# A hybrid decoder layer on one core: the first transfers of the kernel in another order

## The chip, the cores and the metric

The kernel runs on one core of a Trainium2 chip. The metric is the device time of one execution in microseconds (us); the median over several runs is compared. A profile of one execution is read beside it. Its span runs from the first to the last instruction.

## What is computed

The reference is one decoder layer on x of 512 rows and 1024 features: a norm, a mixer with two branches (block-sparse attention and a gated delta rule), a residual, a second norm and a squared-ReLU MLP. What matters here is its beginning only:

```
def rms_norm(x, w):
    y = x * rsqrt(mean(x * x, axis=-1) + 1e-6)
    return y * w

h = rms_norm(x, pre_norm_mix)          # x: 512 x 1024
proj = h @ w_in                        # w_in: 1024 x (3600 + 2 * 1024) columns
...                                    # attention, delta rule, merge, w_out
x = x + rms_norm(y, post_norm_mix)
y = square(relu(rms_norm(x, pre_norm_mlp) @ w_mlp_in)) @ w_mlp_out
return x + rms_norm(y, post_norm_mlp)
```

## The kernel before

Every float32 product is made from three: each operand is split into a high part (rounded to the matmul's own format) and a low part (what is left), and TensorE adds high by high, high by low and low by high. ScalarE makes the high part of each weight tile (`w_hi`), VectorE or GpSimd the low part (`w_lo`). The weights of the projection come in 88 "units" of 256 KB; a unit covers 256 columns for two chunks of 128 features. They go through four buffers `raw[0]` to `raw[3]`.

x comes transposed, in eight chunks of 128 features by 512 rows (`x_t[:, k, :]`, 256 KB each, 2048 bytes for a partition). The norm's weight `wpre` (one column for each chunk, 4 KB in all) is multiplied in before the projection, the row scale after it. So for each chunk k, ScalarE makes `h_hi(k) = x_t * wpre` rounded (`h_part`, L1113 through `copy`), and VectorE makes `h_lo(k) = x_t * wpre - h_hi(k)` (L1492).

The beginning is ordered by hand:

- SP's queue (L555 to L563): chunk 0 of x, the first half of unit 0 (semaphore `w0_in`), the second half of unit 0, and then, for u from 1 to 3, unit u and chunks 2u and 2u + 1. After these come unit 4 and those behind it, with x in its own order (`x_sb`, four transfers) and the small vectors between them.
- ScalarE's queue (L1116, L1117): `wpre`, then chunk 1 of x. Behind these two, ScalarE loads its table and runs one activation on a flag. Then it waits for `wpre`, makes `h_hi(0)`, `h_hi(1)`, the second half of `w_hi` of unit 0, and for each u from 1 to 3 `w_hi` of unit u, `h_hi(2u)`, `h_hi(2u + 1)`.
- VectorE casts the first half of unit 0 itself (L1508), makes its low part, and goes on with `h_lo(0)`, the low part of the second half, `h_lo(1)`, and so on.
- TensorE first runs eight matmuls on a tile of ones (`keep_warm`, L933; the profile counts 16 passes), and then `first_unit(u)`, which takes one chunk at a time: a pair of matmuls on `w_hi` and `h_hi` (L697), a pair on `w_lo` and `h_hi` (L703), a pair on `w_hi` and `h_lo` (L706). From unit 4 on, `unit(u)` waits for the whole unit's low part, which GpSimd makes for most units (L1961).

Of the kernel before, what the change touches and what calls it, by code (L numbers as in the profile page):

```python
# [16 lines left out]
F32 = mybir.dt.float32  # L17
F32R = mybir.dt.float32r
ALU = mybir.AluOpType
# [3 lines left out]
P = 128  # L23
D = 1024
S = 512
NT = S // P
KD = D // P
# [163 lines left out]
    return [(name, i) for u, name, i in STEPS if min(u, U_DN) == unit]  # L191


def program(nc, x, x_by_feature, small_vectors, pre_norm_mix, w_in, w_branch_att, w_branch_dn, w_out,
            post_norm_mix, w_mlp_in, w_mlp_out, post_norm_mlp, out):
    ctx = ExitStack()
    base = (nc.sbuf_base + 63) // 64 * 64
# [2 lines left out]
    def at(name, kb, shape, dt=F32):  # L200
        return nc.alloc_sbuf_tensor_at(name, shape, dt, offset=base + int(kb * KB))


    h_hi = at("h_hi", 0, [P, KD, S], F32R)
    h_lo = at("h_lo", 16, [P, KD, S], F32R)
    raw = at("raw", 32, [P, RAW, 512])
    w_hi = at("w_hi", 40, [P, SPL, 512], F32R)
    w_lo = at("w_lo", 48, [P, SPL, 512], F32R)

    x_t = at("x_t", 56, [P, KD, S])  # L210
    x_sb = at("x_sb", 112, [P, NT, D])
    gate_a = at("gate_a", 56, [P, KD, S])
    qk_dn = at("qk_dn", 72, [P, 8, S])
# [65 lines left out]
    def small(name, shape, dt=F32):  # L279
        n = 4  # L280
        for d in shape[1:]:
            n *= d
        t = nc.alloc_sbuf_tensor_at(name, shape, dt, offset=base + off[0])
        off[0] += (n + 31) // 32 * 32
        return t
# [5 lines left out]
    wpre = small("wpre", [P, KD])  # L291
# [45 lines left out]
    def sem(name):  # L337
        return ctx.enter_context(nc.semaphore(name))

    x_in = [sem(f"x_in{t}") for t in range(NT)]  # L340
    xt_in = [sem(f"xt_in{k}") for k in range(KD)]
# [11 lines left out]
    wpre_in = sem("wpre_in")  # L353
# [3 lines left out]
    w0_in = sem("w0_in")  # L357
# [7 lines left out]
    hhi_ready = sem("hhi_ready")  # L365
    hlo_ready = sem("hlo_ready")
# [108 lines left out]
    def unit_source(u):  # L475

        if u < U_IN:
            g = UNIT_GROUP[u]
            col, kind = GROUPS[g]
            j = u - TABLE[g][0]  # L480
            if kind == "f":
                return w1[j * 256:(j + 1) * 256, col:col + 256].rearrange("(k p) c -> p k c", p=P)
            return w1[j * P:(j + 1) * P, col:col + 512]
        if u < U_BR:
            j = u - U_IN
            w, g = (w_branch_att, w_branch_dn)[j // 8][0], j % 8 // 2
            return w[j % 2 * 256:j % 2 * 256 + 256, g * 256:g * 256 + 256].rearrange("(k p) c -> p k c", p=P)
        j = u - U_BR
        return w_out[0][j // 2 * P:j // 2 * P + P, j % 2 * 512:j % 2 * 512 + 512]
# [52 lines left out]
    def _(sp_):  # L542
# [8 lines left out]
        def load_xt(k):  # L551
            sp_.dma_start(x_t[:, k, :], x_by_feature[k * P:(k + 1) * P, :]).then_inc(xt_in[k], 16)

        load_xt(0)
        sp_.dma_start(raw[:, 0, 0:256], unit_source(0)[:, 0, :]).then_inc(w0_in, 16)  # L555
        sp_.dma_start(raw[:, 0, 256:512], unit_source(0)[:, 1, :]).then_inc(raw_in[0], 16)
        for u in range(1, 4):
            load(u, u, unit_source(u), None)
# [114 lines left out]
    def _(pe):  # L673
# [11 lines left out]
        def first_unit(u):  # L685

            first, banks, _, _ = TABLE[0]
            for kk in range(2):
                k = 2 * u + kk
                c = [slice(kk * 256 + m * P, kk * 256 + m * P + P) for m in range(2)]  # L690
                if k == 0:
                    pe.wait_ge(w0_hi, 1)
                else:
                    pe.wait_ge(hi_ready, u + 1)
                pe.wait_ge(hhi_ready, k + 1)
                for m in range(2):
                    pe.matmul(bank[banks[m]][:], w_hi[:, u, c[m]], h_hi[:, k, :], start=k == 0, stop=False, skip_group_check=True)  # L697
                if k == 0:
                    pe.wait_ge(w0_lo, 1)
                else:  # L700
                    pe.wait_ge(lo_ready, u + 1)
                for m in range(2):
                    pe.matmul(bank[banks[m]][:], w_lo[:, u, c[m]], h_hi[:, k, :], start=False, stop=False, skip_group_check=True)  # L703
                pe.wait_ge(hlo_ready, k + 1)
                for m in range(2):
                    i = pe.matmul(bank[banks[m]][:], w_hi[:, u, c[m]], h_lo[:, k, :], start=False, stop=k == KD - 1,  # L706
                                  skip_group_check=True)
            i.then_inc(unit_done, 1)

        def unit(u):  # L710
            s = u % SPL
            pe.wait_ge(lo_ready, u + 1)
            if u < U_IN:
                g = UNIT_GROUP[u]
                first, banks, _, need = TABLE[g]
                j = u - first
                if GROUPS[g][1] == "f":
# [377 lines left out]
    def _(a):  # L1095
        n = {}

        def mark(i, s):

            n[s.name] = n.get(s.name, 0) + 1  # L1100
            i.then_inc(s, 1)
            a.wait_ge(s, n[s.name])
# [9 lines left out]
        def copy(o, i_, scale=1.0):  # L1112
            return a.activation(o, i_, ACT.Copy, scale=scale)  # L1113


        a.dma_start(wpre[:], pre_norm_mix).then_inc(wpre_in, 16)  # L1116
        a.dma_start(x_t[:, 1, :], x_by_feature[P:2 * P, :]).then_inc(xt_in[1], 16)  # L1117
        a.wait_ge(flag_set, 1)
# [6 lines left out]
        def h_part(k):  # L1125

            a.wait_ge(xt_in[k], 16)
            mark(copy(h_hi[:, k, :], x_t[:, k, :], wpre[:, k:k + 1]), hhi_ready)

        def split(u, slot, loaded, used):  # L1130

# [10 lines left out]
            a.wait_ge(unit_done, U_DN)  # L1142
            copy(wx_hi[:, j, :], raw_x[:, j, :]).then_inc(hix_ready, 1)

        a.wait_ge(wpre_in, 16)
        h_part(0)
        h_part(1)
        a.wait_ge(raw_in[0], 16)
        copy(w_hi[:, 0, 256:512], raw[:, 0, 256:512]).then_inc(hi_ready, 1)
        for u in range(1, 4):  # L1150
            split_u(u)
            h_part(2 * u)
            h_part(2 * u + 1)
# [7 lines left out]
        def side_step(name, i):  # L1161
# [24 lines left out]
            elif name == "sg":  # L1186
                a.wait_ge(conv_done, i + 1)
                dst = qk_dn[:, i, :] if i < 8 else v_dn[:, i - 8, :]
                mark(a.activation(dst, dst, ACT.Silu), silu_done if i < 8 else silu_v_done)
            elif name == "ev" and i in (10, 11):  # L1190
                first, banks, _, _ = TABLE[i]
                for m, b in enumerate(banks):
                    if m < NT - 1:
# [281 lines left out]
    def _(v):  # L1475
        n = {}

        def mark(i, s):
            n[s.name] = n.get(s.name, 0) + 1
            i.then_inc(s, 1)  # L1480
            v.wait_ge(s, n[s.name])
# [9 lines left out]
        def stt(o, i0, s, i1, op0, op1):  # L1491
            return v.scalar_tensor_tensor(out=o, in0=i0, scalar=s, in1=i1, op0=op0, op1=op1)  # L1492
# [7 lines left out]
        def w_lo_part(u, c=slice(0, 512)):  # L1500
            return v.tensor_tensor(w_lo[:, u, c], raw[:, u, c], w_hi[:, u, c].bitcast(F32), ALU.subtract)

        def h_part(k):
            v.wait_ge(hhi_ready, k + 1)
            mark(stt(h_lo[:, k, :], x_t[:, k, :], wpre[:, k:k + 1], h_hi[:, k, :].bitcast(F32), ALU.mult, ALU.subtract), hlo_ready)

        v.wait_ge(w0_in, 16)
        mark(v.tensor_copy(w_hi[:, 0, 0:256], raw[:, 0, 0:256]), w0_hi)  # L1508
        mark(w_lo_part(0, slice(0, 256)), w0_lo)
        v.wait_ge(wpre_in, 16)  # L1510
        h_part(0)
        v.wait_ge(hi_ready, 1)
        w_lo_part(0, slice(256, 512)).then_inc(lo_ready, 1)
        h_part(1)
        for u in range(1, 4):
            v.wait_ge(hi_ready, u + 1)
            w_lo_part(u).then_inc(lo_ready, 1)
            h_part(2 * u)
            h_part(2 * u + 1)
# [13 lines left out]
        def side_step(name, i):  # L1533
# [28 lines left out]
            elif name == "b2":  # L1562
                s3 = [sp[:, q, :] for q in range(6)]
                for c in (9, 7, 5, 3):
# [6 lines left out]
                         alog.unsqueeze(1).to_broadcast([P, NT, H]), ALU.mult, ALU.mult), g_ready)  # L1571
            elif name == "ev" and i not in (10, 11):
                first, banks, _, _ = TABLE[i]
                v.wait_ge(unit_done, first + 4)
                if i == 14:
# [565 lines left out]
```

## Time and profile before

| | |
|---|---|
| time, median of 3 runs | 753.74 us (753.39 to 754.31) |
| the profiled execution | 753.69 us |
| its span | 751.9 us |
| TensorE busy | 744.5 us (99%) |
| VectorE, ScalarE, GpSimd busy | 418.1, 383.9, 322.6 us |
| mean granted TensorE clock | 0.998 |

An engine's busy time counts its own instructions; TensorE's weight loads are counted apart, since they run beside its matmuls. A timeline row gives the start, the length, the engine and line, what is written from what, the count of merged instructions and, in brackets, how long the engine had been idle and what ended that. SPq and ACTq are the queues on which SP and ScalarE issue transfers; the length of such a row is that of the issue alone.

### The profile page before, as it was taken

Reading aid. Unit: us, or ns where it says so; the run is one execution under the profiler, and the core shown is the slowest. Engines: PE = TensorE matmul, PEld = TensorE weight load, DVE = VectorE, ACT = ScalarE, POOL = GpSimd, SP = SyncE. Lnnn points to the kernel's source line nnn. Section 1 sums busy time; section 2 is a strip of 40 time slices with the busy share of each in tenths; the row PEclk is TensorE's granted clock in tenths of the full one; section 3 lists DMA queues with packets and bytes.
Section 4 is the critical chain, followed back from the end, with each engine's and each line's share of the span. In section 5 each row is a group of like instructions: output and inputs, shape, how many; then the busy total and the mean of one; then the engine's idle time right before and its main releaser. Section 6 shows DMA issues by size and latency. Waiting matters only on the chain.

```text
span 751.9 us, 12181 instructions
## 1 busy us (share of the span) xinstructions
PE 744.5 (99%) x4180; PEld 610.3 (81%) x4180; DVE 418.1 (56%) x627; ACT 383.9 (51%) x623; POOL 322.6 (43%) x294
## 2 busy tenths in 40 slices
PE   9999999999999999999999999999999999999996
PEld 7788778888877878788887988888888888888885
DVE  5796899980444545345702612211221777788795
ACT  6656842268554365635524833323332655555671
POOL 2357894435454754575446464445445000000002
PEclk9999999999999999999999999999999999999999
DMA  9336224577596688397941244556484775554652
GB/s 329 112 88 208 56 65 117 156 183 173 165 196 156 188 176 210 100 224 211 287 160 42 71 126 141 130 183 168 129 214 129 202 237 189 194 191 159 208 183 113
DMA packets 83214, 123.45 MB, mean 164 GB/s; under 512 B 5824, under 2 KB 44896, under 8 KB 83168
## 3 DMA queue, kind: packets, MB, share of 16 engines
q1 hardware_dynamic: 74384, 105.80, 43.9%
q0 software_dynamic: 8448, 16.78, 13.1%
q8 instruction: 26, 0.43, 0.2%
q10 hardware_dynamic: 336, 0.28, 0.1%
q14 instruction: 20, 0.16, 0.1%
HBM read 120.73 MB, written 35.67 MB: 208 GB/s over the span
## 4 chain that ended last, share of the span: by engine, by line
PE 93%; POOL 3%; ACT 2%; DVE 1%; issue 0%; ACTq 0%; POOLq 0%; DVEq 0%
PE bank L676 28%; PE bank L678 27%; PE bank L677 27%; POOL rsq L1955 2%; PE bank L901 1%; PE bank L924 1%; PE bank L911 1%; POOL w_lo L1961 1%; PE bank L865 1%; PE bank L829 1%; PE bank L697 1%; PE bank L706 1%; PE bank L876 1%; PE bank L933 1%; PE bank L973 0%; PE bank L703 0%
## 5 line engine op out<-in xcount | busy, mean ns | idle before, releaser
L1961 POOL TENSOR_TENSOR w_lo<-raw,w_hi 128x512 fp32r<-128x512 f32 x177 | 229.5, 1305 | 251.5 <-ACT w_hi L1113 249.7
L1113 ACT ACTIVATE w_hi<-raw 128x512 fp32r<-128x512 f32 (+2 forms) x214 | 144.9, 684 | 171.7 <-PE bank L678 160.1
L676 PE MATMUL bank<-h_hi,w_hi 128*128 128x512 f32 (+1 forms) x528 | 208.5, 395 | 0.1
L677 PE MATMUL bank<-h_lo,w_hi 128*128 128x512 f32 (+1 forms) x528 | 204.2, 387 | 0.0
L678 PE MATMUL bank<-h_hi,w_lo 128*128 128x512 f32 (+1 forms) x528 | 204.1, 386 | 0.0
L676 PEld LDWEIGHTS bank<-h_hi,w_hi 128*128 128x128 f32 x528 | 99.2, 188 | 25.0 <-issue 4.0
L678 PEld LDWEIGHTS bank<-h_hi,w_lo 128*128 128x128 f32 x528 | 99.2, 188 | 20.6
L677 PEld LDWEIGHTS bank<-h_lo,w_hi 128*128 128x128 f32 x528 | 99.3, 188 | 18.7
L1492 DVE SCALAR_TENSOR_TENSOR relu_sb<-bank,rs_row 128x512 f32<-128x512 f32 x32 | 20.6, 686 | 126.5 <-PE bank L678 114.8
L2092 POOL TENSOR_SCALAR ssh<-ssy 128x1 f32<-128x1 f32 x4 | 1.0, 238 | 151.6 <-ACT junk L1463 151.6
L676 PE MATMUL bank<-w_hi,h_hi 128*128 128x512 f32 x128 | 50.3, 393 | 0.1
L678 PE MATMUL bank<-w_hi,h_lo 128*128 128x512 f32 x128 | 49.9, 389 | 0.0
L677 PE MATMUL bank<-w_lo,h_hi 128*128 128x512 f32 x128 | 49.8, 389 | 0.0
L676 PE MATMUL bank<-w_hi,a_hi 128*128 128x512 f32 x120 | 46.8, 390 | 0.0
L678 PE MATMUL bank<-w_hi,a_lo 128*128 128x512 f32 x120 | 46.7, 389 | 0.0
L677 PE MATMUL bank<-w_lo,a_hi 128*128 128x512 f32 x120 | 46.7, 389 | 0.0
L1817 DVE TENSOR_TENSOR w_lo<-raw,w_hi 128x1024 fp32r<-128x1024 f32 (+1 forms) x32 | 37.0, 1157 | 10.9 <-ACT w_hi L1113 10.4
L676 PE MATMUL bank<-wb_hi,a_hi 128*128 128x512 f32 x96 | 37.3, 389 | 0.0
L677 PE MATMUL bank<-wb_lo,a_hi 128*128 128x512 f32 x96 | 37.3, 389 | 0.0
L678 PE MATMUL bank<-wb_hi,a_lo 128*128 128x512 f32 x96 | 37.3, 389 | 0.0
L1350 ACT ACTIVATE act<-relu_sb 128x512 f32 (+1 forms) x28 | 17.4, 632 | 37.8 <-DVE relu_sb L1492 37.3
L1811 DVE TENSOR_TENSOR a_lo<-act,a_hi 128x1024 fp32r<-128x1024 f32 (+1 forms) x27 | 29.5, 1093 | 7.2 <-ACT a_hi L1113 7.2
(300 smaller groups left out, 1204.2 us busy)
## 6 DMA issues: line engine op xcount, KB each, us to landing
raw<-in_w_in SPq DMA_DIRECT2D x87, 256.0 KB, 3.2
raw<-in_w_mlp_in SPq DMA_DIRECT2D x62, 256.0 KB, 2.7
t_sum<-in_w_mlp_out POOLq DMA_DIRECT2D x12, 1024.0 KB, 10.7
raw<-in_w_mlp_out SPq DMA_DIRECT2D x26, 256.0 KB, 3.0
raw<-t_sum SPq DMA_DIRECT2D x26, 256.0 KB, 3.3
v_sum<-in_w_mlp_out SPq DMA_DIRECT2D x4, 1024.0 KB, 7.1
t_sum<-in_w_mlp_out SPq DMA_DIRECT2D x4, 1024.0 KB, 7.1
v_sum<-in_w_mlp_out POOLq DMA_DIRECT2D x4, 1024.0 KB, 11.5
```

The lines of the kernel that those rows point to most:

```text
L676: pe.matmul(o, s_hi, m_hi, start=start, stop=False, skip_group_check=True)
L677: pe.matmul(o, s_hi, m_lo, start=False, stop=False, skip_group_check=True)
L678: return pe.matmul(o, s_lo, m_hi, start=False, stop=stop, skip_group_check=True)
L697: pe.matmul(bank[banks[m]][:], w_hi[:, u, c[m]], h_hi[:, k, :], start=k == 0, stop=False, skip_group_check=True)
L706: i = pe.matmul(bank[banks[m]][:], w_hi[:, u, c[m]], h_lo[:, k, :], start=False, stop=k == KD - 1, skip_group_check=True)
L1113: return a.activation(o, i_, ACT.Copy, scale=scale)
L1350: a.activation(act_pair(i * 2 + q, slice(4, 6) if m else slice(0, 3, 2)), relu_sb[:, 2 * q + m, :].rearrange("p (s c) -> p s c", s=2), ACT ...
L1492: return v.scalar_tensor_tensor(out=o, in0=i0, scalar=s, in1=i1, op0=op0, op1=op1)
L1811: v.tensor_tensor(a_lo[b][:, c], act_row(n, slots), a_hi[b][:, c].bitcast(F32), ALU.subtract).then_inc(alo_ready, 1)
L1817: v.tensor_tensor(l, raw_part(s, n), h.bitcast(F32), ALU.subtract).then_inc(part_lo, n)
L1955: return g.tensor_tensor(dst, src, nhalf[:, 0:width], ALU.pow)
L1961: g.tensor_tensor(w_lo[:, slot, :], raw[:, slot, :], w_hi[:, slot, :].bitcast(F32), ALU.subtract).then_inc(lo_ready, 1)
```

## The change

Column 0 of the norm's weight is put behind each of the 128 rows of chunk 0 in the DRAM input, as element 513, so the two arrive in one transfer of 128 rows of 2052 bytes, in a buffer of its own (`x_first`). `h_hi(0)` and `h_lo(0)` read from it, so neither waits for `wpre`; that wait now stands behind `h_hi(0)` on ScalarE and ahead of `h_lo(1)` on VectorE. The first half of unit 0 moves from second place on SP's queue to the head of ScalarE's, ahead of `wpre` and chunk 1.

```
-        load_xt(0)
-        sp_.dma_start(raw[:, 0, 0:256], unit_source(0)[:, 0, :]).then_inc(w0_in, 16)
+        sp_.dma_start(x_first[:], x_first_rows).then_inc(xt_in[0], 16)
         sp_.dma_start(raw[:, 0, 256:512], unit_source(0)[:, 1, :]).then_inc(raw_in[0], 16)
...
+        a.dma_start(raw[:, 0, 0:256], unit_source(0)[:, 0, :]).then_inc(w0_in, 16)
         a.dma_start(wpre[:], pre_norm_mix).then_inc(wpre_in, 16)
         a.dma_start(x_t[:, 1, :], x_by_feature[P:2 * P, :]).then_inc(xt_in[1], 16)
...
             a.wait_ge(xt_in[k], 16)
-            mark(copy(h_hi[:, k, :], x_t[:, k, :], wpre[:, k:k + 1]), hhi_ready)
+            if k == 0:
+                mark(copy(h_hi[:, 0, :], x_first[:, 0:S], x_first[:, S:S + 1]), hhi_ready)
+                a.wait_ge(wpre_in, 16)
+            else:
+                mark(copy(h_hi[:, k, :], x_t[:, k, :], wpre[:, k:k + 1]), hhi_ready)
...
-        a.wait_ge(wpre_in, 16)
         h_part(0)
...
-            mark(stt(h_lo[:, k, :], x_t[:, k, :], wpre[:, k:k + 1], h_hi[:, k, :].bitcast(F32), ALU.mult, ALU.subtract), hlo_ready)
+            x_, w_ = (x_t[:, k, :], wpre[:, k:k + 1]) if k else (x_first[:, 0:S], x_first[:, S:S + 1])
+            mark(stt(h_lo[:, k, :], x_, w_, h_hi[:, k, :].bitcast(F32), ALU.mult, ALU.subtract), hlo_ready)
...
-        v.wait_ge(wpre_in, 16)
         h_part(0)
         v.wait_ge(hi_ready, 1)
         w_lo_part(0, slice(256, 512)).then_inc(lo_ready, 1)
+        v.wait_ge(wpre_in, 16)
         h_part(1)
...
+        "x_first_rows": np.concatenate([given["x"][0].T[0:P], given["pre_norm_mix"][0].reshape(KD, P).T[:, 0:1]], axis=1),
```

## Rows read from the trace of the kernel before

**Rows 1.** The page: busy time by engine (part 1), the chain that ended last (part 4)

```profile
PE 744.5 (99%) x4180; PEld 610.3 (81%) x4180; DVE 418.1 (56%) x627; ACT 383.9 (51%) x623; POOL 322.6 (43%) x294
...
PE 93%; POOL 3%; ACT 2%; DVE 1%; issue 0%; ACTq 0%; POOLq 0%; DVEq 0%
```

**Rows 2.** Timeline, TensorE: start us, us, engine, line, operation, count, idle before

```profile
1.13 3.78 PE L933 MATMUL bank<-ones 128*128 128x128 f32 x16 [1.13 <-DVE ones L1497]
...
4.89 0.73 PE L697 MATMUL bank<-h_hi,w_hi 128*128 128x512 f32 x2
...
6.13 0.73 PE L706 MATMUL bank<-h_lo,w_hi 128*128 128x512 f32 x2
...
8.25 0.70 PE L697 MATMUL bank<-h_hi,w_hi 128*128 128x512 f32 x2
...
9.71 0.62 PE L697 MATMUL bank<-h_hi,w_hi 128*128 128x512 f32 x2
...
16.07 0.61 PE L706 MATMUL bank<-h_lo,w_hi 128*128 128x512 f32 x2
```

**Rows 3.** Windows: stretch, us, busy by engine, granted clock, DMA share, GB/s

```profile
2.00:2.40 0.40, 0.40 (x4) 0.40 (x4) 0.00 (x0) 0.40 (x1) 0.31 (x2) 1.00 0.40 31
2.40:5.50 3.10, 3.10 (x15) 2.67 (x15) 0.89 (x3) 2.08 (x4) 1.51 (x5) 1.00 1.03 340
9.70:16.60 6.90, 6.90 (x32) 5.56 (x31) 4.80 (x8) 4.93 (x8) 1.29 (x1) 1.00 1.05 392
```

**Rows 4.** Timeline, ScalarE, with what ended the idle time before it

```profile
0.81 0.42 ACTq L1116 DMA_DIRECT2D wpre<-in_pre_norm_mix  x1
...
1.26 0.46 ACTq L1117 DMA_DIRECT2D x_t<-in_x_by_feature  x1
...
3.95 0.72 ACT L1113 ACTIVATE h_hi<-x_t,wpre 128x512 fp32r<-128x512 f32 x1 [0.71 <-DMA wpre<-in_pre_norm_mix]
...
4.97 0.73 ACT L1113 ACTIVATE h_hi<-x_t,wpre 128x512 fp32r<-128x512 f32 x1 [0.30 <-DMA x_t<-in_x_by_feature]
...
5.73 0.42 ACT L1113 ACTIVATE w_hi<-raw 128x256 fp32r<-128x256 f32 x1
...
6.72 0.63 ACT L1113 ACTIVATE w_hi<-raw 128x512 fp32r<-128x512 f32 x1 [0.57 <-DMA raw<-in_w_in]
...
7.38 1.49 ACT L1113 ACTIVATE h_hi<-x_t,wpre 128x512 fp32r<-128x512 f32 x2
```

**Rows 5.** Timeline, SP's queue of transfers

```profile
0.82 0.40 SPq L552 DMA_DIRECT2D x_t<-in_x_by_feature  x1
...
2.21 0.43 SPq L549 DMA_DIRECT2D raw<-in_w_in  x1
```

**Rows 6.** Timeline, unit 4: ScalarE, GpSimd, TensorE's weight load

```profile
14.33 0.63 ACT L1113 ACTIVATE w_hi<-raw 128x512 fp32r<-128x512 f32 x1 [1.28 <-DMA raw<-in_w_in]
...
15.14 1.29 POOL L1961 TENSOR_TENSOR w_lo<-raw,w_hi 128x512 fp32r<-128x512 f32 x1 [10.89 <-ACT w_hi L1113]
...
16.48 0.19 PEld L676 LDWEIGHTS bank<-h_hi,w_hi 128*128 128x128 f32 x1 [0.22 <-POOL w_lo L1961]
```

**Rows 7.** DMA issues between 1.2 and 1.3 us: KB each, us to landing

```profile
x_t<-in_x_by_feature SPq DMA_DIRECT2D x1, 256.0 KB, 2.8
x_t<-in_x_by_feature ACTq DMA_DIRECT2D x1, 256.0 KB, 3.6
```

**Rows 8.** Timeline, VectorE

```profile
4.54 0.29 DVE L1508 CAST w_hi<-raw 128x256 fp32r<-128x256 f32 x1 [3.34 <-DMA raw<-in_w_in]
...
6.25 0.42 DVE L1501 TENSOR_TENSOR w_lo<-raw,w_hi 128x256 fp32r<-128x256 f32 x1 [0.17 <-ACT w_hi L1113]
...
6.59 0.74 DVE L1492 SCALAR_TENSOR_TENSOR h_lo<-x_t,wpre,h_hi 128x512 fp32r<-128x512 f32 x1
```

**Rows 9.** DMA queues, 3.75 to 4.00 us (q10 ScalarE's, q1 SP's)

```profile
q10 hardware_dynamic: 46, 0.09, 96.6%
q1 hardware_dynamic: 21, 0.01, 12.5%
```

More of the change, by code:

```diff
@@ L191, in steps_at, with program @@
     return [(name, i) for u, name, i in STEPS if min(u, U_DN) == unit]
-def program(nc, x, x_by_feature, small_vectors, pre_norm_mix, w_in, w_branch_att, w_branch_dn, w_out,
+def program(nc, x, x_by_feature, x_first_rows, small_vectors, pre_norm_mix, w_in, w_branch_att, w_branch_dn, w_out,
             post_norm_mix, w_mlp_in, w_mlp_out, post_norm_mlp, out):
@@ L210, in program @@
     x_t = at("x_t", 56, [P, KD, S])
+    x_first = at("x_first", 72, [P, S + 1])
     x_sb = at("x_sb", 112, [P, NT, D])
```

## The prediction

> **What bounds the kernel now.** I read the page first. TensorE is busy for 744.5 of the 751.9 us of the span, and 93% of the chain that ended last is TensorE's own work [rows 1]. So an edit of the first microseconds is worth what it moves TensorE's queue as a whole, and no more. The profiled execution took 753.69 us, 1.8 us more than its span, and the median of the three runs shown is 753.74 us, so terms worked out on the span can be added to the median. The three runs spread from 753.39 to 754.31 us; with that spread I take 0.2% (1.5 us) as what a measurement can tell from no change.
>
> Next came the order of events on TensorE in the first 10 us [rows 2]. The warm-up matmuls end at 1.13 + 3.78 = 4.91 us, and the first real pair (weights `w_hi`, chunk 0) starts at 4.89. TensorE's own pace is read between 9.71 and 16.07: 14 pairs in 6.36 us, 0.454 us a pair, so the six matmuls of a chunk take 1.36 us. Chunk 2's pair starts at 8.25, where pace alone from 4.89 would give 4.89 + 2 x 1.36 = 7.61: 0.64 us is lost in waits. From 9.71 on there is no wait: TensorE is busy for 6.90 of 6.90 us [rows 3]. All that the change could win on TensorE is therefore about 0.64 us, plus 0.1 us after 8.25 (chunk 3 starts 1.46 us later, not 1.36): 0.1% of the time. Before 4.89 there is little, since the warm-up stands in the same queue until 4.91.
>
> Then: what ends the waits. ScalarE makes `h_hi(0)` at 3.95 (its wait of 0.71 us is ended by the norm's weight), `h_hi(1)` at 4.97 after chunk 1 lands, the second half of `w_hi` at 5.73, ready by 6.15, and then it waits 0.57 us for unit 1's weights, makes their `w_hi` at 6.72 and `h_hi(2)` from 7.38 (two in 1.49 us, so the first ends near 8.12) [rows 4]. Chunk 2's matmul at 8.25 follows that. So the last wait of the start-up is a transfer: unit 1, issued at 2.21 [rows 5] and used at 6.72.
>
> Why does a transfer of 256 KB take 4.5 us? The windows show it: from 2.40 us the 16 DMA engines are busy for all of the time (share 1.03, 340 GB/s); before that they moved 31 GB/s [rows 3]. From 9.70 to 16.60 they are still full. The transfers stand in line, and issuing one sooner doesn't make it land sooner unless it overtakes another.
>
> The last view is unit 4, the first one after the hand-ordered units 0 to 3. ScalarE waits 1.28 us for its transfer and splits it at 14.33, GpSimd makes `w_lo` from 15.14 to 16.43, and TensorE's weight load, ready 0.22 us earlier, starts at 16.48 [rows 6]. TensorE's own pace would bring it there at 16.07 + 0.46 = 16.53. Both arrive together. **Time won before this point is given back here, unless the stream of transfers itself moves up.**
>
> **The change, part by part.**
>
> *The norm's weight travels with chunk 0.* Removed: the wait for `wpre` ahead of `h_hi(0)`. Chunk 0 was issued at 0.82 [rows 5] and took 2.8 us [rows 7], so it had landed at 3.62; `wpre` came just before 3.95. Taken alone the limit on `h_hi(0)` would be 3.62 + 0.1, a gain of up to 0.23 us.
>
> *The first half of unit 0 leads ScalarE's queue.* It is issued at 0.81, where `wpre` was [rows 4], instead of second on SP's queue; that is the same moment as chunk 0, and both share the engines. 263 KB + 131 KB at 340 GB/s from 2.40 end at 3.56. A tail from last byte to use must be added; chunk 1 of before gives it: 262 + 131 + 4 + 262 KB end at 4.34, and it landed at 1.26 + 3.6 = 4.86 [rows 7], so 0.52 us. Chunk 0 and the half unit then both land near 4.08 (bounds: 3.6 if chunk 0 goes first, 4.1 if last). `h_hi(0)` starts 0.11 us later, as `h_hi(1)` did after its landing, at 4.19, and ends at 4.91: 0.24 us later than in the trace (3.95 + 0.72 = 4.67). `w_hi` of the half is cast (0.29 us) from about 4.15 instead of 4.54 [rows 8] and ends at 4.44. The first real pair starts at about 4.96 instead of 4.89. What is won is behind it: `w_lo` and `h_lo(0)` are then ready in time, so the pair on `h_lo(0)` starts at 4.96 + 2 x 0.46 = 5.88, not at 6.13, and chunk 1 could start at 6.34.
>
> *SP's queue loses one issue.* Everything behind it is issued 0.46 us sooner. Cost and gain nothing: the engines are full from 2.40 on and the bytes ahead of unit 1 are the same, so it still lands for a start at 6.72, and unit 4 for a start at 14.33.
>
> *ScalarE's queue gets one more issue.* `wpre` and chunk 1 are issued 0.45 us later (an issue takes 0.42 to 0.46), and the table load with the flag's activation behind them. ScalarE was free at 3.95 - 0.71 = 3.24 [rows 4]; it is now at 3.70, before chunk 0 lands: hidden, and it would cost up to 0.1 us if chunk 0 landed at 3.6. The moved wait for `wpre` lies behind the copy that ends at 4.9; the 4 KB took 3.95 - 0.81 = 3.1 us and are now issued at 1.26, so they land by about 4.4: nothing.
>
> Chunk 1 is the item that gets later. With chunk 0, both halves of unit 0, `wpre` and itself served, 790 KB take 2.33 us: it lands at 2.40 + 2.33 + 0.52 = 5.25 instead of 4.86. Behind it stand, one after the other: `h_hi(1)` (0.11 + 0.73), the second half of `w_hi` (0.03 + 0.42), its `w_lo` on VectorE (0.10 later), `h_lo(1)` (0.34 + 0.74) [rows 4, 8], the pair on it (0.05 + 0.46) and only then chunk 2. The sum is landing + 2.98 us. For 5.25 it gives 8.23, for 8.25 it gives a limit of 5.27. So the late chunk eats exactly the slack that there is, and chunk 2 starts at 8.25 as before.
>
> **Sum:** 0.25 us won inside chunk 0, nothing at 8.25, nothing at 16.5. Predicted time 753.7 us.
>
> **What a rule would make of chunk 1.** In the window 3.75 to 4.00 us, when chunk 1 on ScalarE's queue met unit 0's halves on SP's, ScalarE's queue had 96.6% of the engines' time and SP's 12.5% [rows 9]; that is why I place chunk 1 ahead of unit 1 although both are now issued at about 1.7 (1.26 + 0.46 and 2.21 - 0.46). The Trainium skill, DMA: Bandwidth & Descriptors, section "Queues, rings and completion order", says that each DMA engine takes turns between the queues that have work, packet by packet. By that rule chunk 1 (2 KB rows) would share with unit 1 (1 KB rows) and not go ahead; the window doesn't look like equal turns. What that would cost is the first rival.
>
> **Rivals.**
>
> *Slower: chunk 1 is passed by unit 1.* If half of unit 1 (131 KB, 0.39 us) is served before chunk 1 has ended, it lands at 5.64, and chunk 2 starts at 5.64 + 2.98 = 8.62: 0.37 us late, all of which stays, since TensorE has no gap later: 754.1 us. If all of unit 1 goes first, landing is at 6.02 and the loss 0.75 us: 754.5 us. It decides from a landing at 5.27 on. For it: the slack is only 0.02 us, and two issues at one moment. Against: rows 9. Chance 0.17.
>
> *Slower: the 2052-byte rows.* Chunk 0's rows in memory no longer start at a multiple of 2048 bytes, and no row of the trace shows such a transfer. Below, the cost is nothing; above, I let the transfer take twice its 0.77 us (262 KB at 340 GB/s): the whole stream is 0.77 us later, 754.5 us. Nearest to it is an ordinary chunk, so I take nothing. Chance 0.03. The same page's section "How a descriptor splits into AXI transactions" has a row that starts off a 256-byte boundary fetch the bytes before its start too; by it the reads of a row grow by some 8% (an estimate), which would be 0.06 us and is not in the sum.
>
> *Faster: the stream moves up.* If unit 1 and those behind it were bound by their issue and not by full engines, all land 0.46 us sooner, unit 4 too, and chunk 2 starts at 4.86 + 2.98 = 7.84: 753.3 us. Against it is the share of 1.03 from 2.40 on [rows 3]. Chance 0.08.
>
> **How the numbers follow.** Forecast (chunk 2 within 0.1 us of 8.25) 0.72, rivals 0.17, 0.03, 0.08. All lie between 753.3 and 754.5; with 0.2 us more on the low side, since the lowest run shown lies 0.35 us under its median, the range is 753.1 to 754.5. No case reaches 1.5 us either way. I leave 0.02 for faster and 0.04 for slower, for what I haven't seen, and 0.94 for no change.
>
> **What would show it.** Right: `h_hi(0)` starts at 4.0 to 4.2, the first real pair at 4.9 to 5.0, the pair on `h_lo(0)` before 6.0, chunk 1 lands at 5.2 to 5.3, chunk 2's pair at 8.2 to 8.3, unit 4's weight load at 16.4 to 16.6. Wrong: chunk 1 landing after 5.4 with chunk 2 after 8.4, or unit 1's split on ScalarE before 6.5 and unit 4's weight load before 16.3.

## The result, and the profile after

The change makes the kernel slower: 756.05 us in the median (755.30 to 758.72, 8 runs) against 753.74 us (753.39 to 754.31, 8 runs), a ratio of 1.0034 with the interval [1.0024, 1.0043]. The loss of 2.31 us lies above my range (753.1 to 754.5) and above the 0.2% that I had given 0.04. The profiled execution took 755.3 us, the fastest of its eight, 1.61 us more than that of before (753.69). In the experiments below two executions were far slower than all others (827.67 us of `one_less`, and 1065.24 us of before beside it); leaving them out moves no median by more than 0.01 us.

The page of after (busy time, and the chain that ended last) looks as in [rows 1]:

```profile
PE 744.8 (99%) x4180; PEld 610.2 (81%) x4180; DVE 418.9 (56%) x627; ACT 383.7 (51%) x623; POOL 322.6 (43%) x294
...
PE 93%; DVE 5%; ACT 1%; DMA 1%; issue 0%; POOL 0%; ACTq 0%; DVEq 0%; POOLq 0%
```

TensorE's work is 0.3 us longer in a span that is 1.7 us longer, so the loss is waiting. "DVE 5%" (VectorE's share of that chain) where before had 1% is a first hint that time is lost in a second place too. Timeline of after, the first 10 us, the rows that answer to [rows 2, 4, 8]:

```profile
1.73 0.45 ACTq L1118 DMA_DIRECT2D x_t<-in_x_by_feature  x1
...
4.32 0.72 ACT L1113 ACTIVATE h_hi<-x_first 128x512 fp32r<-128x512 f32 x1 [0.61 <-DMA x_first<-in_x_first_rows]
...
4.57 0.29 DVE L1513 CAST w_hi<-raw 128x256 fp32r<-128x256 f32 x1 [3.37 <-DMA raw<-in_w_in]
...
5.19 0.70 PE L697 MATMUL bank<-h_hi,w_hi 128*128 128x512 f32 x2 [0.27 <-ACT h_hi L1113]
...
6.19 0.71 PE L706 MATMUL bank<-h_lo,w_hi 128*128 128x512 f32 x2
...
6.21 0.72 ACT L1113 ACTIVATE h_hi<-x_t,wpre 128x512 fp32r<-128x512 f32 x1 [1.16 <-DMA x_t<-in_x_by_feature]
...
7.43 0.73 PE L697 MATMUL bank<-h_hi,w_hi 128*128 128x512 f32 x2 [0.53 <-ACT w_hi L1113]
...
9.19 0.63 PE L697 MATMUL bank<-h_hi,w_hi 128*128 128x512 f32 x2
```

The reader is to see three things. The first pair is 0.30 us later (5.19 for 4.89) and the pair on `h_lo(0)` 0.06 later, so nothing was won inside chunk 0. Chunk 1 is used 1.24 us later (6.21 for 4.97). Chunk 2 starts 0.94 us later (9.19 for 8.25). The DMA issues of after between 0 and 7 us (KB, us from issue to landing; before in [rows 7]) say the same of the transfers:

```profile
x_first<-in_x_first_rows SPq DMA_DIRECT2D x1, 256.5 KB, 3.4
x_t<-in_x_by_feature ACTq DMA_DIRECT2D x1, 256.0 KB, 4.4
raw<-in_w_in ACTq DMA_DIRECT2D x1, 128.0 KB, 3.7
```

Chunk 1 was issued at 1.73 and landed 4.4 us later, near 6.13, where I had 5.25. Unit 4 in the timeline of after, against [rows 6]:

```profile
13.96 0.63 ACT L1113 ACTIVATE w_hi<-raw 128x512 fp32r<-128x512 f32 x1 [0.62 <-DMA raw<-in_w_in]
...
14.77 1.48 POOL L1966 TENSOR_TENSOR w_lo<-raw,w_hi 128x512 fp32r<-128x512 f32 x1 [10.52 <-ACT w_hi L1113]
...
17.16 0.19 PEld L676 LDWEIGHTS bank<-h_hi,w_hi 128*128 128x128 f32 x1
```

Unit 4's data are there 0.37 us sooner, but TensorE comes 0.68 us later (17.16 for 16.48) and is the last.

The windows of after that answer to two of [rows 3] (us, busy by engine, granted clock, DMA share, GB/s):

```profile
2.40:5.50 3.10, 2.83 (x14) 2.52 (x14) 0.86 (x3) 2.03 (x3) 1.51 (x5) 1.00 1.03 335
9.70:16.60 6.90, 6.90 (x32) 5.64 (x31) 6.17 (x9) 5.46 (x10) 1.48 (x1) 1.00 1.06 392
```

The DMA engines are as full as before (335 GB/s for 340): they did the same work in another order, and chunk 1 had the later place. From 9.70 on TensorE has no wait again, so most of what was lost by then stays lost: chunk 2 is 0.94 us late, and from 30 us on TensorE is 0.76 us behind before.

**The second place** is 120 us further on. TensorE's offset between the two traces is 0.76 us just ahead of the unit that starts at 136.26 us in before (a matmul at 136.51 for 135.75), and 1.57 us behind its first matmuls (138.70 for 137.13). In the table of waits, between 124 and 139 us, after has a line that before lacks (us in all, times, longest):

```profile
PEld bank L676 <- DVE qk_att L1589: 1.1, 2, 1.0
```

TensorE waits for a PSUM bank that VectorE empties into `qk_att`. VectorE is late because of what happened 8 us earlier (L1589, L1634 of after are L1584, L1629 of before). Timeline of before:

```profile
127.45 0.63 ACT L1113 ACTIVATE w_hi<-raw 128x512 fp32r<-128x512 f32 x1 [2.37 <-PE bank L678]
...
128.04 0.41 DVE L1629 TENSOR_TENSOR t_rows<-t_rows,prod 128x240 f32<-128x240 f32 x1
128.16 1.43 POOL L1961 TENSOR_TENSOR w_lo<-raw,w_hi 128x512 fp32r<-128x512 f32 x1 [1.71 <-ACT w_hi L1113]
128.48 1.42 DVE L1584 TENSOR_TENSOR qk_att<-bank,rs_row_x 128x512 f32<-128x512 f32 x2
```

And of after:

```profile
127.92 0.63 ACT L1113 ACTIVATE w_hi<-raw 128x512 fp32r<-128x512 f32 x1 [2.08 <-PE bank L678]
...
128.63 1.29 POOL L1966 TENSOR_TENSOR w_lo<-raw,w_hi 128x512 fp32r<-128x512 f32 x1 [1.42 <-ACT w_hi L1113]
128.81 1.38 DVE L1634 TENSOR_TENSOR t_rows<-t_rows,prod 128x240 f32<-128x240 f32 x1
130.22 1.42 DVE L1589 TENSOR_TENSOR qk_att<-bank,rs_row_x 128x512 f32<-128x512 f32 x2
```

This is weight unit 40, the 41st that is split (GpSimd makes its low part). In before the VectorE operation on `t_rows` had started 0.12 us ahead of GpSimd and took 0.41 us, and GpSimd's operation was drawn out a little (1.43 us for 1.29); in after it starts 0.18 us behind GpSimd and ends only when GpSimd has been done for 0.27 us (128.63 + 1.29 = 129.92, 128.81 + 1.38 = 130.19). The Trainium skill, SBUF — State Buffer, section "SBUF: two separate sides", says that a VectorE operation with two SBUF inputs and a GpSimd operation that reads SBUF lock each other out for a whole instruction; the traces agree (1.38 for 0.41 us), and the product that reads a PSUM bank beside GpSimd takes 1.42 us for two in both. Being held is nothing rare: between 124 and 135 us three of VectorE's operations take 1.39 or 1.40 us in before. In after four take 1.25 to 1.42 us; the fourth is the loss.

Why did the order turn round? TensorE's offset is 0.76 us here, and VectorE's is 0.77 (128.81 for 128.04), but ScalarE's copy comes only 0.47 us later (127.92 for 127.45). In before, 3.00 us lie between the copies of units 39 and 40 (124.45, 127.45) and 2.44 to the next; in after, 2.71 and 2.73. **So in before this copy was 0.28 us late, and that lateness is gone in after.** What had made it late was to be found.

### The profile page after: what moved, and what is told of

It is laid out like the page before. It is cut to its first block, busy times and chain, and to the rows that moved or that the text cites. A ratio compares the mean times of both kernels' runs of the same rounds, so it can differ in the third digit from the quotient of the medians.

```text
span 753.6 us, 12182 instructions
## 1 busy us (share of the span) xinstructions
PE 744.8 (99%) x4180; PEld 610.2 (81%) x4180; DVE 418.9 (56%) x627; ACT 383.7 (51%) x623; POOL 322.6 (43%) x294
## 4 chain that ended last, share of the span: by engine, by line
PE 93%; DVE 5%; ACT 1%; DMA 1%; issue 0%; POOL 0%; ACTq 0%; DVEq 0%; POOLq 0%
PE bank L676 28%; PE bank L678 27%; PE bank L677 27%; PE bank L901 1%; DVE prod L1632 1%; DVE t_rows L1634 1%; PE bank L924 1%; PE bank L911 1%; PE bank L814 1%; PE bank L865 1%; DMA x_t<-in_x_by_feature 1%; PE bank L829 1%; PE bank L876 1%; PE bank L973 0%; PE bank L805 0%; PE bank L697 0%
```

## The experiments

**The two halves of the change alone.** `x_only` keeps `x_first` and the moved waits, and puts the half unit back in second place on SP's queue:

```
         sp_.dma_start(x_first[:], x_first_rows).then_inc(xt_in[0], 16)
+        sp_.dma_start(raw[:, 0, 0:256], unit_source(0)[:, 0, :]).then_inc(w0_in, 16)
...
-        a.dma_start(raw[:, 0, 0:256], unit_source(0)[:, 0, :]).then_inc(w0_in, 16)
```

> One part alone: chunk 0 and its column of the norm's weight in one transfer of 2052-byte rows; the first half of unit 0 stays second on SP's queue and ScalarE's queue holds wpre and chunk 1, as before. Theory A (the loss comes from chunk 1, third on ScalarE's queue and taking turns with SP's transfers): chunk 1 lands by 5.0 us, chunk 2's first matmul starts at 8.2 to 8.3, and the time is that of before, 753.5 to 754.1. Theory B (the 2052-byte rows are slow or push the stream back): a good part of the loss stays, chunk 2 at 8.7 or later and 755 us or more.

`lead_only` is before with only the half unit moved to the head of ScalarE's queue:

```
         load_xt(0)
-        sp_.dma_start(raw[:, 0, 0:256], unit_source(0)[:, 0, :]).then_inc(w0_in, 16)
...
+        a.dma_start(raw[:, 0, 0:256], unit_source(0)[:, 0, :]).then_inc(w0_in, 16)
         a.dma_start(wpre[:], pre_norm_mix).then_inc(wpre_in, 16)
```

> The other part alone: the first half of unit 0 at the head of ScalarE's queue, ahead of wpre and chunk 1; chunk 0 in ordinary 2048-byte rows and h_hi(0) waiting for wpre. Theory A: chunk 1 lands near 6.1 us as in the changed kernel, chunk 2 starts at 9.1 to 9.2, the time is 755.3 to 756.5. Theory B: chunk 1 lands by 5.3, time within 0.3 us of before.

Measured: `x_only` 753.68 us, ratio 1.0002 [0.9993, 1.0011]; `lead_only` 756.92 us, ratio 1.0046 [1.0032, 1.006]. The loss is all in the moved half unit. The rows of 2052 bytes cost nothing that could be measured, and the norm's weight in the transfer of chunk 0 gives nothing: in `x_only` chunk 2 starts as in before, in its timeline:

```profile
8.24 0.62 PE L698 MATMUL bank<-h_hi,w_hi 128*128 128x512 f32 x2
```

`lead_only` is 3.30 us over before, more than after and more than I had expected. Its chunk 1 landed 5.3 us after its issue at 1.73, near 7.0 and not at 6.1, and its first matmuls were slow (more on them under "What stays open").

**Chunk 1 ahead of `wpre`.** `x1_before_wpre` swaps the last two issues on ScalarE's queue, so that chunk 1 is issued at 1.25 again:

```
         a.dma_start(raw[:, 0, 0:256], unit_source(0)[:, 0, :]).then_inc(w0_in, 16)
-        a.dma_start(wpre[:], pre_norm_mix).then_inc(wpre_in, 16)
         a.dma_start(x_t[:, 1, :], x_by_feature[P:2 * P, :]).then_inc(xt_in[1], 16)
+        a.dma_start(wpre[:], pre_norm_mix).then_inc(wpre_in, 16)
```

> The changed kernel with chunk 1 issued before wpre on ScalarE's queue (half unit, chunk 1, wpre). Theory A: the 128 tiny packets of wpre no longer stand between, each of which lets a packet of SP's queue pass, so chunk 1 lands 0.4 to 0.6 us earlier (5.5 to 5.7), chunk 2 starts at 8.5 to 8.7 and the time falls by 0.4 us or more against the changed kernel (756.05), to 754.2 if the later loss goes too. Theory B: the time stays at 755.5 to 756.5.

Measured: 755.13 us, ratio 1.0020 [1.0011, 1.003], 1.51 us over the before of its job where after has 2.31. Chunk 1 landed at 1.25 + 4.0 = 5.25, but the wait had only changed its name (timeline, ScalarE):

```profile
6.00 0.72 ACT L1113 ACTIVATE h_hi<-x_t,wpre 128x512 fp32r<-128x512 f32 x1 [1.11 <-DMA wpre<-in_pre_norm_mix]
```

Third place on ScalarE's queue is late for a transfer of 4 KB as well as for one of 256.

**Is the second loss a matter of being late?** `shift2` and `shift4` are before with 2 or (`range(4)`) 4 more matmuls on the tile of ones behind unit 3; the rest of TensorE's work comes later by their length:

```
+        for _ in range(2):
+            pe.matmul(bank[3][:, 0:P], ones[:], ones[:], start=True, stop=True)
```

> The kernel before, with two more matmuls on the tile of ones (four passes, into a bank that is not in use) behind the matmuls of unit 3, so that TensorE alone is pushed back by about 0.95 us at 16.5 us and no transfer is changed. Theory C (a shift of about 0.8 us is multiplied later, where VectorE's chain of the triangular solve meets GpSimd's low parts at another phase): 755.3 to 756.5, with a second wait of TensorE of 0.5 to 1 us near 137 us. Theory D (the second loss comes from the transfers of the change, their order or their place in memory, not from the shift): 754.6 to 754.8, the shift alone.

> The kernel before with four more matmuls on the tile of ones behind unit 3 (eight passes of about 0.11 us, going by shift2, where four passes cost some 0.45 us). TensorE is pushed back by 0.65 to 0.9 us at unit 4; no transfer is changed. Theory C (between a shift of 0.2 and 0.5 us there is a step: VectorE meets one more of GpSimd's low parts and TensorE waits 0.95 us for qk_att near 137 us): 755.1 to 755.6. Theory D (the second loss belongs to the changed transfers): 754.3 to 754.6.

Measured: 754.05 us, ratio 1.0006 [0.9997, 1.0015], and 754.69 us, ratio 1.0013 [1.0004, 1.0021]: 0.43 and 1.04 us over before in the same job. In the traces the added matmuls take 0.36 us (from 16.36 to 16.72) and 0.80 us (from 16.26 to 17.06), for the 0.95 that I had expected of `shift2`; so the time is about what the delay itself is, and the wait at 136 us isn't there. That a late TensorE alone brings the second loss on was a theory of mine, and it fell.

**Is it GpSimd's work on unit 40?** `cut40` is after, but GpSimd makes only 8 of the 512 columns of unit 40's low part; the other 504 are left out.

```
+            c = slice(0, 8) if isinstance(ready, int) and ready == nth(40) else slice(0, 512)
-            g.tensor_tensor(w_lo[:, slot, :], raw[:, slot, :], w_hi[:, slot, :].bitcast(F32),
+            g.tensor_tensor(w_lo[:, slot, c], raw[:, slot, c], w_hi[:, slot, c].bitcast(F32),
```

> The changed kernel, in which GpSimd makes only 8 of the 512 columns of unit 40's low part (the rest of that low part is left out), so that its instruction at 128.6 us is short and VectorE's product of the triangular solve that started 0.18 us later and took 1.38 us isn't held. Theory C (one held VectorE instruction is the whole second loss): that instruction takes 0.41 us, TensorE has no wait near 137 us and the time falls by 0.9 to 1.0 us, to 755.1. Theory D: the wait stays, time 755.8 to 756.3.

Measured: 755.22 us, ratio 1.0018 [1.0009, 1.0027]: 1.57 us over the before of its job where after has 2.31, TensorE has no wait at 136 us, and the product takes its usual time (timeline, VectorE):

```profile
129.58 0.41 DVE L1634 TENSOR_TENSOR t_rows<-t_rows,prod 128x240 f32<-128x240 f32 x1
```

**Would more warm-up help the start?** `more_warm` is after with two more warm-up matmuls (`keep_warm(10)`).

> The changed kernel with ten warm-up matmuls in place of eight (about 0.95 us more, up to 5.85 us, where chunk 1's first matmul can't start before 7.4). Theory E (in some executions TensorE's idle time ahead of chunk 0 keeps its matmuls at half pace for the first microseconds, which makes the median 0.7 us worse than the profiled execution of the changed kernel): median 755.1 to 755.5. Rival (the spread has another cause): median as the changed kernel's, 755.9 to 756.2.

Measured: 756.00 us, ratio 1.0030 [1.0019, 1.0041]. That is 2.35 us over before for 2.31: no difference to after. More warm-up wins nothing, and that theory fell.

**Chunk 1 on SP's queue.** `x1_on_sp` issues it second there, behind `x_first`; ScalarE's queue keeps the half unit and `wpre`, two issues as in before:

```
         sp_.dma_start(x_first[:], x_first_rows).then_inc(xt_in[0], 16)
+        load_xt(1)
...
-        a.dma_start(x_t[:, 1, :], x_by_feature[P:2 * P, :]).then_inc(xt_in[1], 16)
```

> The changed kernel with chunk 1 second on SP's queue, right behind chunk 0, instead of third on ScalarE's; the half unit and wpre stay on ScalarE's queue. Theory A (only chunk 1's landing matters): it lands at 4.7 to 5.2 us, the second half of unit 0 by 5.6, chunk 2 starts at 8.1 to 8.4 and the time is that of before, 753.4 to 754.1. Rival (any transfer at the head of ScalarE's queue delays the stream): 754.5 or more.

Measured: 753.70 us, ratio 1.0000 [0.9992, 1.0009]. Both losses are gone from the median together. Chunk 1 was issued at 1.27 and landed at 5.07, and the timeline has:

```profile
5.31 0.73 ACT L1114 ACTIVATE h_hi<-x_t,wpre 128x512 fp32r<-128x512 f32 x1 [0.17 <-DMA wpre<-in_pre_norm_mix]
```

In this profile (753.81 us) chunk 2 still starts 0.34 us later than in before, at 8.59, since the first pair came at 5.28; from there to chunk 2 no wait of TensorE is shown, and of the 0.34 only 0.12 us is left at 30 us.

That the *second* loss went too pointed at something that this kernel shares with before: ScalarE's program has 823 instructions in both, and 824 in after. (This is my own count. The traces' records of ScalarE, counted whole, are 1150 in both and 1151 in after; the difference of one is the same.)

**One instruction more on ScalarE, and nothing else.** `pad1` is before with a wait that is already met (824 instructions); `pad2` has the added line three times, which makes two instructions more than before (825):

```
+        a.wait_ge(ones_set, 1)
         a.wait_ge(flag_set, 1)
```

`one_less` is after with 823: the activation on the flag signals nothing.

```
-        link(a.activation(flag[:], flag[:], ACT.Square))
+        a.activation(flag[:], flag[:], ACT.Square)
```

> The kernel before with one instruction more on ScalarE, a wait that is already met, ahead of the flag's activation; transfers, shift and everything else unchanged. In all ten traces so far the wait of TensorE near 137 us goes with the count of ScalarE's instructions: 823 without it, 824 (a third transfer issued there) with it. Theory F (one instruction more moves the place at which ScalarE's next 8 KB of instructions are fetched, so unit 40's high part isn't late by 0.28 us any more, and GpSimd's low part then catches one more of VectorE's products): the time is 754.5 to 754.8, 0.95 us over before, with the wait near 137 us. Theory C (the wait comes from the shift of the start): 753.5 to 753.9, no wait.

> The changed kernel with one instruction less on ScalarE: the flag's activation no longer signals, so that the separate wait behind it goes. The three transfers on ScalarE's queue stay. Theory F: ScalarE's 40th unit stands where it stood before the change, the wait near 137 us goes, and only the late chunk 1 is left: 754.9 to 755.4. Theory C: nothing changes, 755.8 to 756.3.

> The kernel before with two instructions more on ScalarE (waits that are already met, at the head). Each unit is a wait and the copy behind it. Theory F (the 190th instruction of ScalarE's stream is the first of a newly fetched block and comes 0.28 us late; it is unit 40's copy in the kernel before, unit 40's wait with one instruction more, and with two more unit 39's copy): unit 39's copy now comes 0.28 us late (3.9 us behind unit 38's instead of 3.6), and the distance from 39 to 40 is 2.4 us. The time follows from which of VectorE's products are then held, which I can't say: 753.3 to 754.8. Rival (any instruction more removes the pause): distances as in pad1, 3.6 and 2.7, time 754.3.

Measured: `pad1` 754.33 us, ratio 1.0008 [0.9999, 1.0017], 0.75 us over before, where I had expected 0.95, with no loss at the start (chunk 1 again 3.6 us after its issue). The interval just includes no change, but all 11 executions (754.12 to 754.69) lie above 30 of the 33 of before. In its table of waits, 124 to 139 us:

```profile
PEld bank L676 <- DVE qk_att L1585: 1.1, 2, 0.9
```

`pad2` 754.31 us, ratio 1.0011 [1.0002, 1.002], and it has the wait. `one_less` 755.12 us, ratio 1.0016 [1.0007, 1.0025], and it doesn't. So the instruction count switches the second loss on and off, with the start as it was.

The traces say so more sharply than the medians. Matched with before matmul by matmul, all eight traces that have one or two instructions more on ScalarE, and GpSimd's work whole, fall back by another 0.8 to 0.9 us between 135 and 139 us, however early or late TensorE comes there: `pad1` and `pad2` are 0.34 and 0.38 us ahead of before at 135 us, `x1_before_wpre` 0.59, after 0.76, `after_c` 0.65, `more_warm` 1.51, `lead_only` 2.52 and `after_b` 3.53 us behind. The seven others, with as many instructions as before, 0.21 us ahead of it to 1.73 us behind, change by at most 0.04 us there. That rules the lateness of the start out as the cause.

In `pad2` the late copy is that of unit 39 (timeline, ScalarE):

```profile
120.47 0.63 ACT L1113 ACTIVATE w_hi<-raw 128x512 fp32r<-128x512 f32 x1 [2.09 <-PE bank L678]
124.36 0.63 ACT L1113 ACTIVATE w_hi<-raw 128x512 fp32r<-128x512 f32 x1 [3.26 <-PE bank L678]
126.80 0.63 ACT L1113 ACTIVATE w_hi<-raw 128x512 fp32r<-128x512 f32 x1 [1.81 <-PE bank L678]
```

3.89 us from unit 38's copy to unit 39's and then 2.44; in before these are 3.61 (120.84 to 124.45) and 3.00. The lateness sits at a place in ScalarE's code, not at a unit. Counted in the traces, unit 40's copy is ScalarE's 190th instruction in before and the 191st in `pad1`; in `pad2` the 190th is unit 39's copy.

**Both keys at once.** `pad1_cut40` is `pad1` with the cut of `cut40` (504 columns of unit 40's low part left out).

> pad1 with only 8 of 512 columns of unit 40's low part made by GpSimd (the rest is left out). If the held product is the whole loss of pad1, the wait near 137 us goes and the time is that of before, 753.3 to 753.7. If the extra instruction costs something of its own, it stays near 754.3.

Measured: 753.48 us, ratio 1.0000 [0.9991, 1.0009]. The one instruction costs its 0.75 us only through GpSimd's work on unit 40: the traces of `pad1_cut40` and `cut40` change by at most 0.02 us between 135 and 139 us.

**Other orders.** `x1_second` is after with `wpre` third on SP's queue (ScalarE: half unit, chunk 1). `x_only_x1_first` has `x_first` and both halves of unit 0 on SP's queue, and chunk 1 ahead of `wpre` on ScalarE's. The edit of `x1_second`:

```
         sp_.dma_start(raw[:, 0, 256:512], unit_source(0)[:, 1, :]).then_inc(raw_in[0], 16)
+        sp_.dma_start(wpre[:], pre_norm_mix).then_inc(wpre_in, 16)
...
-        a.dma_start(wpre[:], pre_norm_mix).then_inc(wpre_in, 16)
```

> The changed kernel with wpre on SP's queue, third, behind the second half of unit 0, so that ScalarE's queue holds the half unit and chunk 1 alone (823 instructions). Theory A with F: chunk 1 is issued at 1.25 us, still takes turns, and lands at 5.2 to 5.8; the wait near 137 us is gone; 753.7 to 754.5. Rival (a half unit at the head of the queue costs whatever follows): 755 or more.

> A version that might beat both: chunk 0 with its column, both halves of unit 0 on SP's queue, and on ScalarE's queue chunk 1 ahead of wpre. Chunk 1 lands by 4.6 us, wpre by 5.0, so chunk 1's work is never late. If what is left is TensorE's pace from the first pair on, chunk 2 starts at 7.9 to 8.1 and the time is 753.2 to 753.5; if unit 1's landing (about 6.4 to 6.7 us) sets chunk 2, it stays at 753.5 to 753.8.

Measured: 753.93 us, ratio 1.0005 [0.9996, 1.0014], and 753.71 us, ratio 1.0001 [0.9992, 1.001]. Neither beats before. In `x1_second` chunk 1 landed at 1.25 + 4.1 = 5.35, and chunk 2 starts at 8.59 as in `x1_on_sp`.

**The spread of after itself.** `after_b` and `after_c` are the kernel after, profiled once more each.

> The changed kernel once more, for a second profile. If chunk 1's landing is what differs between executions, its landing is 4.4 to 5.3 us after its issue and the time of the profiled execution follows it: 755.3 with 4.4, 756.0 to 756.4 with 5.1 to 5.3. Rival (another place differs): the landing is 4.4 and the time 756 or more.

> As after_b, a third profile of the changed kernel: the same relation of landing and time.

Measured: 758.04 and 755.12 us, chunk 1 landing 5.9 and 4.3 us after its issue at 1.73. The first profile had 4.4 and 755.3 us. With `cut40`, `more_warm` and `one_less`, which have the same transfers, there are six profiles, here in the order of chunk 1's landing (issue at 1.73 plus time to landing; all in us):

| profile | chunk 1 lands | chunk 2's first matmul | unit 4's first matmul |
|---|---|---|---|
| before (1.26 + 3.6) | 4.86 | 8.25 | 16.52 |
| `after_c` | 6.03 | 9.09 | 17.31 |
| after | 6.13 | 9.19 | 17.38 |
| `cut40` | 6.83 | 9.95 | 18.15 |
| `more_warm` | 6.83 | 9.94 | 18.13 |
| `one_less` | 7.03 | 10.14 | 18.35 |
| `after_b` | 7.63 | 11.51 | 20.18 |

What is lost at the start follows the landing, and chunk 2 starts 3.06 to 3.12 us behind it in all but the last. What spreads the landing is open. In `after_b` the DMA engines moved only 273 GB/s between 4.0 and 6.5 us at a DMA share of 0.89, and from 6.50 to 7.25 us only 1 or 2 packets of ScalarE's queue start in each quarter of a microsecond: the last rows of chunk 1 trail behind. Why isn't shown.

In `after_b` there follow (timeline, TensorE; windows: us, busy by engine, granted clock, DMA share, GB/s):

```profile
8.92 1.09 PE L697 MATMUL bank<-h_hi,w_hi 128*128 128x512 f32 x2 [1.88 <-ACT w_hi L1113]
```

```profile
9.00:10.00 1.00, 1.00 (x3) 0.77 (x4) 1.00 (x2) 1.00 (x2) 0.00 (x0) 0.55 1.05 389
```

TensorE stood idle for 1.88 us, and from 9 to 10 us its granted clock is 0.55 of full speed, near the 1.2 GHz level, so that a pair lasts 1.09 us and not 0.73. Unit 4 starts at 20.18 there, 2.80 us later than in the first profile.

## Why the prediction was wrong

**What held.** The kernel is bound by TensorE, and a delay of its queue at unit 4 is paid in full (`shift4`: 0.80 us in the trace, 1.04 in the median). Chunk 2's start is the landing of chunk 1 + 2.98 us, to 0.14 us: 6.13 + 2.98 = 9.11, measured 9.19; with the landing at 5.1 us after the issue in `cut40`, 6.83 + 2.98 = 9.81 for 9.95. The rows of 2052 bytes cost nothing measurable (`x_only`).

**What wasn't tested.** The limit of 5.27: in `x1_on_sp` (landing 5.07) and `x1_second` (5.35) chunk 2 starts at 8.59 alike, later than either landing + 2.98 (8.05 and 8.33); in `x1_on_sp` the late first pair (5.28) set it. "Time won before this point is given back here": after came late to unit 4. In `pad1`, whose transfers are those of before, unit 4's first matmul starts at 16.26 for 16.52, so one profile places this point only to about 0.3 us.

**The first wrong step is "it lands at 2.40 + 2.33 + 0.52 = 5.25".** It landed at 6.03 and 6.13 in the two fastest profiles and at 7.63 in the slowest, past both ends of the rival "chunk 1 is passed by unit 1" (5.64 and 6.02). The rival had the right mechanism in that chunk 1 did not keep ahead of unit 1; its size was too small and its chance of 0.17 far too low. I had rejected it on [rows 9]: 96.6% for ScalarE's queue against 12.5% for SP's. I read that as precedence. SP's queue simply had little to send then. Another line of the view of [rows 9] counts the small packets:

```profile
DMA packets 67, 0.10 MB, mean 410 GB/s; under 512 B 13, under 2 KB 21, under 8 KB 67
```

ScalarE's 46 packets with 0.09 MB are rows of 2 KB, so the 21 under 2 KB are those of SP's queue: 13 under 512 bytes and only 8 rows of 1 KB. A quarter of a microsecond earlier the queues of before (packets, MB, share of 16 engines) show

```profile
q10 hardware_dynamic: 29, 0.06, 67.0%
q1 hardware_dynamic: 33, 0.03, 37.5%
```

and after, at 4.75 to 5.00 us, while chunk 1 is on its way:

```profile
q10 hardware_dynamic: 30, 0.06, 63.0%
q1 hardware_dynamic: 30, 0.03, 34.5%
```

That is turn by turn, 30 packets each, as the Trainium skill, DMA: Bandwidth & Descriptors, section "Queues, rings and completion order", says, which I had cited and set aside. The section gives a packet some 9 to 17 descriptors, though; here the turns look shorter. In before, at 2.7 to 3.0 us, the 32-byte pieces of `wpre` (128 in all, so 8 for each of the 16 engines if they share evenly) run beside as many rows of chunk 0, and aren't done in one turn:

```profile
q1 hardware_dynamic: 56, 0.11, 98.0%
q10 hardware_dynamic: 55, 0.00, 10.3%
```

Two things follow from the turns. Chunk 1, issued 0.47 us later, meets unit 1 and the chunks behind it in full, and in turns of a single row one of theirs goes ahead of each of its own. And `wpre`, now second on the same queue, takes turns too: at 3.75 to 4.00 us of after

```profile
q1 hardware_dynamic: 89, 0.08, 95.5%
q10 hardware_dynamic: 96, 0.01, 27.2%
```

ScalarE's queue spends 96 turns on 0.01 MB, nearly all of them 32-byte pieces of `wpre`, while SP's moves 0.08 MB. In bytes `wpre` is nothing, and I had costed it so; in turns it is 128 packets, as many as the half unit. How much of the delay is each one's isn't shown: in `x1_before_wpre` chunk 1 landed 4.0 us after its issue for 4.3 to 5.9, but it was issued 0.48 us sooner too. The order as a whole (half unit, `wpre`, chunk 1) is what the runs show to be late.

**The second is "ScalarE's queue gets one more issue ... hidden, nothing".** I had costed the issue's 0.45 us on its queue, and that was hidden. Not costed was that everything behind it in ScalarE's code moves by one instruction. A pause of 0.28 us at its 190th instruction (unit 40's copy in before and `one_less`; in after and `pad1` that copy is the 191st) then no longer falls on this copy: in `pad2` it falls on unit 39's, and in after and `pad1` no copy near it is late. GpSimd starts 0.3 us sooner against the rest, gets in first, and VectorE, then TensorE, pay 0.75 us (0.75 in `pad1`, 0.77 in `pad2`, nothing in `pad1_cut40`).

**The sum in medians.** With the second loss taken away, `one_less` and `cut40` are 1.54 and 1.57 us over the before of their jobs: that is the start. With `pad1`'s 0.75 it makes 2.3 us, as measured (2.31). In the profiled execution the offset is 0.86 us at unit 4 (17.38 for 16.52, the first matmul's start), 0.76 ahead of the second place, 1.57 behind it, and 1.61 in the time. The median's start (1.54) is dearer than the profile's (0.86) because the profile is the fastest execution: over the six profiles above unit 4 is 0.79 to 1.83 us late for landings of 6.03 to 7.03, and 3.66 us in `after_b`. The prediction had no term for this spread. It also took all of chunk 2's lateness to stay; in the profile of after 0.76 of 0.94 us did.

**Smaller terms.** `h_hi(0)` was forecast at 4.19 and came at 4.32, since `x_first` took 3.4 us beside the half unit, for 2.9 in `x_only`. The prediction has the DMA engines full from 2.40 us on, with 340 GB/s; in after they moved 217 GB/s between 2.4 and 3.0 us, for 339 in before. "`w_hi` of the half is cast from about 4.15" failed: it came at 4.57 for 4.54 before; the half unit, issued 0.46 us sooner, landed no sooner. So the first pair came at 5.19 and not at 4.96. "SP's queue loses one issue: nothing" was wrong by 0.37 us (unit 4 at 13.96 for 14.33), but nothing waited for it.

**What stays open.** The pause moves with the code and not with the work; that is shown. What it is, isn't. The trace has a packet of 8 KB on the instruction queue close by, in before between 128 and 129 us:

```profile
q14 instruction: 1, 0.01, 1.9%
```

and in after between 126 and 127 us:

```profile
q14 instruction: 1, 0.01, 2.0%
```

in `pad1` it lies between 125 and 126. So the packet moves with the one instruction too, and ScalarE's code coming in blocks, with a stop at a block's edge, would fit. But it was only argued: whose code the packet holds isn't shown, and in before it starts after the late copy has begun (127.45), so it is not what that copy waited for. In `lead_only` the matmuls of the first two chunks last some 1.05 us a pair (0.90 to 1.22) while the granted clock reads 1.00; why isn't known.

## What to carry to other kernels

Two DMA queues with work shared the engines turn by turn here: count a transfer's packets, and those of the queue beside it, and not its bytes alone; a window in which one queue has nearly all the time says nothing before it is clear that the other had something to send. A transfer of many tiny rows ahead of the critical one on its queue takes as many turns as one of as many large rows; what that cost here was not separated. One profile of a kernel whose executions spread shows one landing of several: after's first was among the two cheapest of six. And an edit that adds an instruction to an engine can move a fixed pause in its code onto another instruction; where a kernel's engines meet within 0.2 us of each other, a pad of one harmless instruction in the kernel before shows whether a small difference is the edit's own or only the phase.

## What the hardware showed that I had not expected

- One transfer in third place on a queue landed 4.3, 4.4, 5.1, 5.1, 5.3 and 5.9 us after its issue in six profiles of kernels with the order of transfers of after; the two transfers in first place took 3.4 and 3.7 us in after.
- One ScalarE instruction that does nothing, some 120 us ahead of the place, costs 0.75 us (`pad1`), and the cost goes when 504 columns of one GpSimd operation are left out (`pad1_cut40`).
- A VectorE product of two SBUF operands goes from 0.41 to 1.38 us when GpSimd starts 0.18 us ahead of it.
- TensorE's idle time of 1.88 us that ends at 8.92 in `after_b` was followed by a granted clock of 0.55 (9 to 10 us). One of 1.54 us that ends at 8.37 in `one_less` was not (1.00 from 8.37 to 15 us), nor was one of 0.53 us that ends at 7.43 in after (1.00 from 7.40 to 9.70 us, and from 9.70 to 16.60).
